# A chunked two-way recurrence on TensorE: 64x64 products on the crossed quarters of the array beside the straight ones, and decays ahead of keys in the stage before it

## The reference

```
def wkv7_scan(r, decay, k, v, kk_neg, kk_b, reverse):
    def step(state, inp):
        r_t, w_t, k_t, v_t, an_t, b_t = inp
        sa = einsum('bhij,bhj->bhi', state, an_t)
        state = state * w_t + sa[..., None] * b_t + v_t[..., None] * k_t
        return state, einsum('bhij,bhj->bhi', state, r_t)
...
for direction, reverse in ((0, False), (1, True)):
    w_log = -softplus(-(w0[direction] + tanh(wd) @ w_lora_up[direction])) - 0.5
    decay = exp(-exp(w_log))
    a = sigmoid(a0[direction] + ad @ a_lora_up[direction])
    k_dir = k * (1.0 + (a - 1.0) * k_a)
    y = y + wkv7_scan(r, decay, k_dir, v, -kk, kk * a, reverse)
```

## Time and profile before

| | |
|---|---|
| median of 3 runs | 5456.74 us (5455.51 to 5463.51) |
| the profiled execution, its own time | 5460.31 us |
| its span, first to last instruction | 5458.5 us |
| TensorE busy (records) | 4692.6 us, 86% |
| VectorE busy | 3104.5 us, 57% |
| ScalarE busy | 2090.0 us, 38% |
| GpSimd busy | 1089.2 us, 20% |
| `rwkv_inputs` | about 1390 to 2055 us of the span |
| `recurrence` | about 2085 to 3275 us of the span |

### The profile page before, as it was taken

The page is one execution under the profiler, slowest core; times in us unless marked ns, Lnnn a source line. Parts: engine busy times, 40 slices in busy tenths (PEclk is TensorE's granted clock), DMA queues, the critical chain, the costliest instruction groups (busy, mean ns, idle before and its releaser), DMA issues. The chain is left out here.

```text
span 5458.5 us, 141686 instructions
## 1 busy us (share of the span) xinstructions
PE 4692.6 (86%) x60038; PEld 4316.4 (79%) x60038; DVE 3104.5 (57%) x6054; ACT 2090.0 (38%) x4040; POOL 1089.2 (20%) x829
## 2 busy tenths in 40 slices
PE   6878888886788877999999997881299999999998
PEld 5757666664677776999999995661199999999998
DVE  6867777775677774444444444556644444444443
ACT  3347777774455551111111111220044343434343
POOL 4432222221233332000000212210010101010100
PEclk9989999998899998999999998995599999999999
DMA  7810000000433322212122114430155555555553
GB/s 156 155 45 15 14 12 16 12 12 25 153 124 124 123 100 93 61 50 62 50 62 61 50 53 148 148 129 5 41 168 159 170 159 170 166 164 167 163 160 111
DMA packets 496709, 526.44 MB, mean 96 GB/s; under 512 B 74224, under 2 KB 434672, under 8 KB 496240
## 3 DMA queue, kind: packets, MB, share of 16 engines
q1 hardware_dynamic: 390256, 413.95, 23.8%
q10 hardware_dynamic: 92480, 62.93, 5.0%
q0 software_dynamic: 13504, 42.30, 3.5%
HBM read 372.12 MB, written 146.99 MB: 95 GB/s over the span
## 5 line engine op out<-in xcount | busy, mean ns | idle before, releaser
L2185 DVE TENSOR_TENSOR g_wlo<-g_raw,g_whi 128x2048 fp32r<-128x2048 f32 x192 | 439.1, 2287 | 129.6 <-ACT g_whi L2147 129.6
L615 PE MATMUL sapS<-KT,saq 128*128 128x512 f32 x1024 | 369.3, 443 | 123.0 <-ACT saprob L515 115.1
L2147 ACT ACTIVATE g_whi<-g_raw 128x2048 fp32r<-128x2048 f32 x192 | 365.8, 1905 | 246.3 <-DMA g_raw<-expert_w_gate 246.3
L568 DVE TENSOR_REDUCE samx<-sapS 128x1 f32<-128x512 f32 x512 | 352.5, 689 | 184.1 <-PE sapS L615 178.6
L2252 PE MATMUL g_pD<-g_whi,g_hh 128*128 128x256 f32 (+1 forms) x1536 | 437.4, 285 | 0.6
L2252 PE MATMUL g_pD<-g_whi,g_hl 128*128 128x256 f32 (+1 forms) x1536 | 429.4, 280 | 0.0
L2252 PE MATMUL g_pD<-g_wlo,g_hh 128*128 128x256 f32 (+1 forms) x1536 | 429.3, 279 | 0.0
L1426 DVE TENSOR_TENSOR d_zy<-d_zy,d_pZ 128x128 f32<-128x128 f32 x720 | 178.0, 284 | 416.2 <-PE d_pZ L1465 416.0
L523 ACT ACTIVATE saph<-sapT 128x512 fp32r<-128x512 f32 x512 | 305.8, 598 | 225.6 <-PE sapT L630 219.2
L505 POOL TENSOR_SCALAR saprob<-saprob,sarden 128x2048 f32<-128x2048 f32 x128 | 254.8, 1990 | 654.5 <-DVE sarden L587 654.5
L1115 PE MATMUL c_pP<-c_xh,c_whi 128*128 128x258 f32 x1120 | 343.2, 306 | 43.1 <-DMA c_gup<-g_lora_up 27.8
(11 more groups left out here) (383 smaller groups left out, 13246.1 us busy)
## 6 DMA issues: line engine op xcount, KB each, us to landing
g_raw<-expert_w_gate SPq DMA_DIRECT2D x64, 1024.0 KB, 5.3
g_raw<-expert_w_up SPq DMA_DIRECT2D x64, 1024.0 KB, 5.4
g_raw<-expert_w_down SPq DMA_DIRECT2D x64, 1024.0 KB, 5.2
ops<-c_ops SPq DMA_DIRECT2D x40, 1024.0 KB, 4.0
d_bd<-ops SPq DMA_DIRECT2D x80, 512.0 KB, 4.2
c_xh<-xT_hi SPq DMA_DIRECT2D x10, 1032.0 KB, 6.3
c_xl<-xT_lo SPq DMA_DIRECT2D x10, 1032.0 KB, 8.6
x_in<-x SPq DMA_DIRECT2D x20, 512.0 KB, 7.9
```

The source lines that it names most:

```text
L568: ins = dve.tensor_reduce(mx[:, h % 2, k:k + 1], pS[k][:], AX.X, ALU.max)
L615: mm = pe.matmul(pS[k][:], q[:, h // GH, h % GH, :], KT[:, 2 * (h // GH) + p, key0 + k * 512:key0 + (k + 1) * 512], start=(p == 0), stop=( ...
L2147: act.activation(w_hi[:, Q % NBUF, :, :], raw[:, Q % NRAW, :, :], ACT.Copy).then_inc(s["g_hi"], 1)
L2185: dve.tensor_tensor(w_lo[:, Q % NBUF, :, :], raw[:, Q % NRAW, :, :], w_hi[:, Q % NBUF, :, :].bitcast(F32), ALU.subtract).then_inc(s["g_lo" ...
```

## The change

In `recurrence`, `between`, `grown` of Z, `through`, `solved` and a new product x4 now write the other half: the matmul that reads partitions 0 to 63 writes PSUM partitions 64 to 127, and the other way round. So Y, P, `pm`, `zs` of head h lie on the half of the other head, and `grown` of Y reads and writes there. On the array these are the crossed quarters (rows 0 to 63 with columns 64 to 127, rows 64 to 127 with columns 0 to 63), where the products of before are the straight ones. Crossed and straight products are put into the list by turns, pair by pair, for each direction. Y no longer starts from a part of x1 but from x4 (B with A, crossed, to pZ): 8 more matmuls a direction and chunk. Y's increments go to the upper half of bank pP. `values` moves ahead of `turned`. VectorE handles state(0) between the two masks of level 1, and state(1) after that level's additions.

```
-            def products(out, *terms):
+            def heads(cross, out, l, r, first=True, last=True):
+                for h in range(2):
+                    mm = pe.matmul(out(halves[1 - h if cross else h]), l(halves[h]), r(halves[h]), start=first, stop=last)
+                return mm
...
+            def begin(m, par, i, g, n=None):
+                can_begin(m, par, i, g)
+                if n is not None:
+                    can_through(n, g)
                 for j in range(RT):
+                    mm = x1(par, g, j)
+                    if n is not None:
+                        through(1 - par, g, 2 * j)
+                        side = through(1 - par, g, 2 * j + 1)
...
+                can_x3(m, g)
+                for j in range(RT):
+                    mm = x3(par, g, j)
+                    side = x4(par, g, j)
...
+            def keys(m, par, g, n=None):
+                pe.wait_ge(s["d_br"], 2 * m + g + 1)
+                if n is not None:
+                    can_solve(n, g)
+                for j in range(RT // 2):
+                    x2(par, g, j)
+                    if n is not None:
+                        solved(1 - par, g, 2 * j)
+                        side = solved(1 - par, g, 2 * j + 1)
...
+                can_between(m, 0, g)
+                for j in range(RT // 2):
+                    mm = x2(par, g, RT // 2 + j)
+                    between(par, g, 0, 2 * j)
+                    side = between(par, g, 0, 2 * j + 1)
...
+            def grown(m, par, l, g):
+                pe.wait_ge(s["d_Pe"], 2 * (NL * m + l) + g + 1)
+                for j in range(RT):
+                    if l < NL - 1:
+                        side = grown_z(par, g, l, j)
+                    mm = grown_y(par, g, l, j)
...
+            def state_and_between(n, m, par, g):
+                pe.wait_ge(s["d_uc"], 2 * n + g + 1)
+                for i in range(RT):
+                    state(1 - par, g, i)
+                can_between(m, 1, g)
+                for j in range(RT):
+                    mm = state(1 - par, g, RT + j)
+                    side = between(par, g, 1, j)
...
# VectorE, begin: both directions' br first before; now br, then Z, Y of one direction
-                    dve.tensor_tensor(zy[par][g][:, :, 1, :], br[par][g][:, :, 0, :], bc(beside[:, 1 - g, 0:1, :], [P, RT, C]), ALU.mult)
+                    dve.tensor_tensor(zy[par][g][:, :, 1, :], slim(pZ[g]), bc(beside[:, 1 - g, 0:1, :], [P, RT, C]), ALU.mult)
```

`values_and_between` (level 2), `out_and_between` (level 3: eight pairs of `out` alone, then four beside `between`) and `turned_and_between` (level 4) are built like `state_and_between`. In `rwkv_inputs` only the order changes:

```
# ScalarE, slot
-                mid(n, 1)
                 exps(q, 1)
+                mid(n, 1)
# VectorE, slot
                 decays(q, 0)
+                decays(q, 1)
+                shift(n, 0)
                 keys_b(q, 0)
                 keys_a(q, 0)
                 keys_c(q, 0)
-                shift(n, 0)
-                decays(q, 1)
+                if n % 2 == 0:
+                    shift(n, 1)
                 keys_b(q, 1)
-                shift(n, 1)
                 keys_a(q, 1)
                 keys_c(q, 1)
+                if n % 2:
+                    shift(n, 1)
# TensorE, slot, n even
                     tile(n, 4)
-                    bonus(q)
                     tile(n, 5)
                     norms(n)
+                    bonus(q)
                     lora(n, 0)
```

More of the change, by code:

```diff
@@ L1357, in turn @@
-            def turn(n, par, i, more):
-                through(n, par, i)
-                if more:
-                    keys(n + 1, 1 - par)
-                solved(n, par, i)
-                if more:
-                    turned(n + 1, 1 - par)
-                out(n, par, i)
-                if more:
-                    values(n + 1, 1 - par)
-            keys(0, 0)
-            turned(0, 0)
-            values(0, 0)
+                    if more:
+                        turned(n + 1, 1 - par, g)
@@ L1371, in _ @@
+            for g in range(2):
+                keys(0, 0, g)
+            for g in range(2):
+                values(0, 0, g)
+            for g in range(2):
+                turned(0, 0, g)
             with act.Fori(0, NCH // 2 - 1) as i:
@@ L1429, in state, with between @@
[L1429 to L1435 removed]
+            def between(m, l, g):
+                dve.wait_ge(s["d_P"], 2 * (NL * m + l) + g + 1)
+                mask = cols4(beside[:, g, l + 1:l + 2, :], l, g)
+                dve.tensor_tensor(cols4(pm[l][g][:], l, g), packed4(slim(pP[g])[:, :, 0:C // 2], l), bc(mask, [P, RT] + list(mask.shape[2:])), ALU.mult)\
+                   .then_inc(s["d_Pe"], 1)
@@ L1452, in _ @@
             turn(NCH - 2, 0)
-            state(NCH - 1, 1)
+            for g in range(2):
+                state(NCH - 1, 1, g)
         @block.tensor
@@ new lines, in _ @@
+            for g in range(2):
+                begin(0, 0, 0, g)
+            for g in range(2):
+                keys(0, 0, g)
+            for g in range(2):
+                grown(0, 0, 0, g)
+            for g in range(2):
+                between_alone(0, 0, 1, g)
+            for g in range(2):
+                grown(0, 0, 1, g)
+            for g in range(2):
+                values_and_between(0, 0, g)
+            for g in range(2):
+                grown(0, 0, 2, g)
+            for g in range(2):
+                between_alone(0, 0, 3, g)
@@ L1484, in keys @@
+            for g in range(2):
+                grown(0, 0, 3, g)
+            for g in range(2):
+                turned_and_between(0, 0, g)
+            for g in range(2):
+                grown(0, 0, 4, g)
+            for n in range(NCH - 1):
+                m, par = n + 1, (n + 1) % 2
+                for g in range(2):
+                    begin(m, par, m // 2, g, n)
                 for g in range(2):
-                    pe.wait_ge(s["d_br"], 2 * m + g + 1)
-                    products(lambda h, j: wide(pX[g])[h, j, :, :], (op(par, g, OP_K), both(par, g))).then_inc(s["d_x2"], 1)
@@ L1517, in through @@
[L1517 to L1525 removed]
+                    grown(m, par, 1, g)
@@ L1541, in turn @@
-            def turn(n, par, i):
-                m, other = n + 1, 1 - par
-                begin(m, other, i + par)
-                through(n, par)
-                keys(m, other)
-                between(m, other, 0)
-                solved(n, par)
-                grown(m, other, 0)
-                between(m, other, 1)
-                state(n, par)
-                grown(m, other, 1)
-                between(m, other, 2)
-                turned(m, other)
-                grown(m, other, 2)
-                between(m, other, 3)
-                out(n, par)
-                grown(m, other, 3)
-                between(m, other, 4)
-                values(m, other)
-                grown(m, other, 4)
@@ L1562, in _ @@
-            begin(0, 0, 0)
-            keys(0, 0)
-            turned(0, 0)
-            values(0, 0)
-            for l in range(NL):
-                between(0, 0, l)
-                grown(0, 0, l)
-            for n in range(NCH - 1):
-                turn(n, n % 2, n // 2)
-            through(NCH - 1, 1)
-            solved(NCH - 1, 1)
-            state(NCH - 1, 1)
-            out(NCH - 1, 1)
+                    turned_and_between(m, par, g)
+                for g in range(2):
+                    grown(m, par, 4, g)
@@ new lines, in _ @@
+            n, par = NCH - 1, (NCH - 1) % 2
+            for g in range(2):
+                can_through(n, g)
+                for i in range(2 * RT):
+                    mm = through(par, g, i)
+                mm.then_inc(s["d_zs"], 1)
+            for g in range(2):
+                can_solve(n, g)
+                for j in range(RT):
+                    mm = solved(par, g, j)
+                mm.then_inc(s["d_u"], 1)
+            for g in range(2):
+                pe.wait_ge(s["d_uc"], 2 * n + g + 1)
+                for i in range(2 * RT):
+                    mm = state(par, g, i)
+                mm.then_inc(s["d_sn"], 1)
@@ L1577 @@
+            for g in range(2):
+                pe.wait_ge(s["d_tmp"], 2 * n + g + 1)
+                for i in range(3 * RT):
+                    mm = out(par, g, i)
+                mm.then_inc(s["d_yo"], 1)
 NE = 16
```

310 lines of the change are left out of this document (191 added, 119 removed).

## The result

| | before | changed |
|---|---|---|
| median | 5457.12 us (5455.51 to 5463.51, 4 runs) | 5388.84 us (5380.35 to 5400.45, 4 runs) |
| span of the profiled execution | 5458.5 us | 5391.5 us |
| TensorE busy | 4692.6 us, 86% | 4389.7 us, 81% |
| a turn of `recurrence` | 29.67 us | (3176.72 - 2075.96) / 38 = 28.97 us |
| two slots of `rwkv_inputs` | 64.9 us | 61.4 us |

The ratio is 0.9874, 95% interval 0.9852 to 0.9896: 68 us faster, where the prediction had 437. The recurrence, from its first `d_br` to its last, gained (3238.14 - 2087.17) - (3176.72 - 2054.25) = 28.5 us; 32.9 us were gained before it began, and the other 5.6 of the span's 67 behind it.

A forecast was written before the change was run, and what follows sets the result against it. It took TensorE to bound `recurrence` and waits to decide `rwkv_inputs`. From 5460.3 us it took 356 (turns of 20.3 instead of 29.67), 4 (first chunk) and 77 (stage before): 5023, against the median 5020 us; range 4950 to 5385.

The forecast's parts named there:

- What bounds the kernel: `recurrence` is TensorE's, busy 1160.90 of 1195.00 us; in `rwkv_inputs` no engine is full and waits decide.
- Crossed products free beside straight ones: In `recurrence`, a crossed pair beside a straight one costs near zero; upper bound a full 0.0584 us.
- TensorE's work is the straight pairs: 16.8 us: In a turn of `recurrence`, only straight pairs count: 2 x (16 x 0.115 + 112 x 0.0584) = 16.8 us.
- because eight instructions must go out in 0.058 us: Allowance of 0.3 us added to a turn of `recurrence` for handing out instructions at twice today's rate.
- starts 0.01 us apart show that the sequencer can hand out faster: Argument for free crossed pairs: `c_pX` and `c_pY` start 0.01 us apart, so faster than 29 ns a record is possible.
- Waits that come up: In a turn of `recurrence`, thinner cover exposes VectorE's answers: 0.4, 0.3, 0.7 and 1.1, sum 2.5 us.
- Clock 1.00: Sign that the forecast is right: TensorE's granted clock stays at 1.00, the 2.4 GHz level.
- The stage before: `rwkv_inputs`: two slots of 64.9 us get 8.5 us shorter, nine times, 77 us; bounds 45 and 115.
- (a): `rwkv_inputs`, even slots: the tile goes ahead of `bonus`, removing VectorE's 6.06 us wait; 6.1 us a pair of slots.
- (b): `rwkv_inputs`: second scan moved ahead of GpSimd's products gains 4.8 us a pair of slots; keys' operations give back 2.2.
- no gain in the recurrence: Rival, chance 0.15: one column half's weights at a time, or 29 ns a record; turns 28 to 29.5, total 5345 to 5385 us.
- The slower rival: Chance 0.09: about 208 quarter changes a turn each empty the array; at 0.08 us each, turn 45.4 us, total 5980.

The follow-up runs named there:

- e15_best2: Changed kernel with loads spread, bonus later, rwkv_inputs' VectorE and ScalarE order as before, no x4, Y started from PSUM by VectorE: 5318.57 us, ratio 0.9744.

## Why the prediction was wrong

- *What bounds the kernel*: "this stage is TensorE's" was half of it. Beside the array's 3.74 us for 64 straight products stood a second limit of almost the same height, the fetch of the same 256 instructions, and in 23 of 38 turns it bound already (the 25 us that spread loads brought to the kernel before). The rows showed pairs of records 0.0584 us apart without gaps and could not tell the two. I had read q8's packets in the page as bytes, 0.5% of the DMA engines, and not as a pace.
- *Crossed products free beside straight ones*: right. Four records in 0.0584 us, 14.4 against 26.0 us, and 18.4 us of records a turn against the 16.8 of the sum.
- *"TensorE's work is the straight pairs: 16.8 us"* is the step that failed. For the array it holds nearly, but the sum had no term for the supply of instructions: 7.25 packets of 3.98 us, 28.9 us, of which TensorE stands still for some 10. Each product left its place in the array and kept its four instructions, and x4 added 64 a turn. The 0.3 us "because eight instructions must go out in 0.058 us" were my whole allowance; in a burst it is even true, for 128 records at a time.
- *"starts 0.01 us apart show that the sequencer can hand out faster"*: true of a burst, and no row for a sustained pace.
- *Waits that come up*, 2.5 us: not tested as a sum, since the stops cover most of them. The waits for `d_zy` at the turn's start and for `d_pm` were there, 8.1 and 18.7 us in all, under the forecast. At 20.3 us they might have come out.
- *Clock 1.00*: wrong, 0.89. It came with the stops (0.86 in the window from 2617.40 us, which holds most of a stop of 3.2 us); what it costs by itself was not measured.
- *The stage before*: (a), 6.1 us of two slots, was right: nine times 6.1 = 55 us forecast, 50 measured. In (b) the term "the keys' operations give back between nothing and 3.6; I take 2.2" was mis-sized. Three of their groups got (45.0 + 36.0 + 35.1) - (28.3 + 14.1 + 14.7) = 59.0 us longer, 5.9 in two slots. The part came out as a loss of 11 us by itself, and of some 18 us next to (a), instead of a gain of 23. So the stage before gained 33 us where 77 were forecast.
- *The rivals*: the turn was that of "no gain in the recurrence", 28 to 29.5 us, and the time missed its 5345 to 5385 by 4 us at the upper end. That nearness is partly luck: with the 77 us of the stage before, turns of 28 to 29.5 us come to 5317 to 5374, not 5345 to 5385, and the measured turn to 5354; the stage before gained less than half of its 77. Of its two mechanisms the first, a row half that loads weights for one column half at a time, is wrong; the second, records that keep the pace of 29 ns, is right as a mean (3.77 / 128 = 29.4 ns, without loads) and wrong as a mechanism: it is the fetch. Its "against", that 128 columns cost more, spoke of the array and not of this. The slower rival was far off: 208 changes of quarter a turn cost nothing that can be seen. Its two figures also started from different turns, 0.06 us from the forecast's 20.3 and 0.08 from 27.1 + 1.7, where 20.3 + 16.6 would have been 36.9.

## What to carry to other kernels

Where a list is written out and an engine's instructions are short, count them: divide the engine's instructions in a stretch by 256 and compare the stretch with that many fetches, which started 3.4 to 4.1 us apart here. Where the two are about equal, an edit that lets the array work on more at once gains little (28.5 of 360 us here) unless it also has fewer instructions, or the list is a loop that is kept (1600 instructions were, here). Transfers in large bursts hold fetches up; split over the work, the same bytes cost less.

## What was not expected of the hardware

- Fetches of 256 instructions of TensorE start 3.4 to 4.1 us apart even with the DMA engines idle, though a packet moves for only 1.1 us, and TensorE, with all four quarters at work, uses them up in about 2 and stops.
- A loop of 1600 instructions on TensorE ran its second to fourth pass without a fetch. A turn pair of this kernel, 3712 instructions, wasn't tried as a loop.
- A semaphore increment as an instruction of its own costs TensorE 0.10 to 0.11 us between matmuls.
- VectorE operations with both operands in SBUF took twice as long beside GpSimd (1.83 against 0.85 us for two of 64x256). With an operand in PSUM they kept their time: in e15_best2 11 of the 160 operations of 64x256 overlap GpSimd and take 0.43 us, the others 0.42.
